# Holding SyncE's queue until a slot's diagonal blocks have landed, in a DeltaNet and attention layer

## The reference

```python
def _layer(x, w_in, conv_w, a_log, dt_bias, norm_w, sinks, w_out, ln_g, ln_b):
    h = jnp.einsum('btd,dc->btc', x, w_in)
    qa, ka, va, za, ba, aa, qb, kb, vb, zb = jnp.split(h, offsets, axis=-1)
    ya = _deltanet_group(qa, ka, va, za, ba, aa, conv_w, a_log, dt_bias, norm_w)
    yb = _swa_group(qb, kb, vb, zb, sinks)
    y = jnp.einsum('btc,cd->btd', jnp.concatenate([ya, yb], axis=-1), w_out)
    return _layernorm(DEEPNORM_ALPHA * x + y, ln_g, ln_b)

# in the DeltaNet, for each head and chunk of tokens
    a_mat = jnp.where(strict, jnp.einsum('bhncd,bhnsd->bhncs', k_beta, k) * decay, 0.0)
    t_mat = lax.linalg.triangular_solve(eye + a_mat, jnp.broadcast_to(eye, a_mat.shape),
                                        left_side=True, lower=True)
```

## Time and profile before

| | |
|---|---|
| median of 3 runs | 1107.68 us (1106.04 to 1107.72) |
| the profiled execution | 1107.0 us |
| its span, first to last instruction | 1105.1 us |
| PE busy | 1068.7 us, 97% |
| DVE, ACT, POOL busy | 690.8, 533.5, 124.4 us |
| mean granted clock | 0.997 |
| DMA moved | 183.54 MB, mean 166 GB/s |

### The profile page before, as it was taken

How to read it: one execution, slowest core, us unless ns; L and a number is a source line. 1 busy time by engine, 2 the same in 40 slices (tenths; PEclk the granted TensorE clock), 3 DMA queues, 4 the chain that set the end, 5 groups by cost and what they waited for, 6 DMA issues and landing times. The chain is left out here.

```text
span 1105.1 us, 19521 instructions
## 1 busy us (share of the span) xinstructions
PE 1068.7 (97%) x7212; PEld 851.5 (77%) x7212; DVE 690.8 (63%) x2077; ACT 533.5 (48%) x1557; POOL 124.4 (11%) x164
## 2 busy tenths in 40 slices
PE   7999999999999999999999999999999999999997
PEld 5877777867878787877877878787786868787885
DVE  5285959585565848576365765848447474758564
ACT  4466565654735444463354536444454545463310
POOL 3413222133200000020000000002000000002330
PEclk9999999999999999999999999999999999999999
DMA  8766575655652726253453461724444343612331
GB/s 274 275 245 231 205 252 201 230 182 182 224 197 85 247 81 222 95 183 101 168 190 126 155 219 53 254 78 153 147 160 153 126 153 126 228 58 60 133 113 77
DMA packets 58285, 183.54 MB, mean 166 GB/s; under 512 B 8464, under 2 KB 21200, under 8 KB 44880
## 3 DMA queue, kind: packets, MB, share of 16 engines
q1 hardware_dynamic: 51392, 173.13, 45.0%
q10 hardware_dynamic: 6800, 9.18, 2.8%
HBM read 138.22 MB, written 44.07 MB: 165 GB/s over the span
## 5 line engine op out<-in xcount | busy, mean ns | idle before, releaser
L821 PE MATMUL bank<-xr,w 128*128 128x512 f32 x2496 | 653.7, 405 | 8.7 <-DVE xr L1507 7.6
L821 PEld LDWEIGHTS bank<-xr,w 128*128 128x128 f32 x2496 | 451.7, 189 | 106.9 <-issue 13.0
L872 PE MATMUL bank<-wo,y_split 128*128 128x512 f32 x432 | 114.3, 404 | 0.0
L872 PEld LDWEIGHTS bank<-wo,y_split 128*128 128x128 f32 x432 | 77.1, 188 | 15.6 <-issue 1.7
L1555 DVE SCALAR_TENSOR_TENSOR kq<-conv_in,convw_all,kq 128x512 f32<-128x512 f32 x96 | 75.6, 787 | 9.1 <-ACT conv_in L1160 7.1
L1320 ACT ACTIVATE score<-score,neg_max 128x256 f32<-128x256 f32 (+1 forms) x128 | 62.6, 491 | 20.7 <-DVE neg_max L1725 20.7
L1879 DVE TENSOR_SCALAR steps<-bank,nb_rk 128x128 f32<-128x128 f32 x64 | 22.4, 351 | 78.0 <-PE bank L1084 78.0
L1458 ACT ACTIVATE o_scaled<-bank 128x128 f32<-128x128 f32 x64 | 17.6, 275 | 98.6 <-PE bank L1088 98.2
L1759 DVE TENSOR_TENSOR y_step<-blocks,y_cols 128x60 f32<-128x60 f32 (+14 forms) x240 | 50.5, 210 | 20.4 <-DMA blocks<-n_spill 12.0
L1882 DVE SCALAR_TENSOR_TENSOR state<-state,cols_all,bank 128x128 f32<-128x128 f32 x64 | 22.1, 345 | 60.4 <-PE bank L1087 60.3
L754 POOL TENSOR_TENSOR xr<-y_tile,xr 128x256 fp32r<-128x256 f32 x8 | 6.0, 775 | 456.7 <-ACT xr L1141 456.7
(11 more groups left out here) (218 smaller groups left out, 1642.7 us busy)
## 6 DMA issues: line engine op xcount, KB each, us to landing
w<-w_split SPq DMA_DIRECT2D x78, 1024.0 KB, 5.6
w_split<-w SPq DMA_DIRECT2D x26, 1024.0 KB, 5.3
blocks<-n_spill ACTq DMA_DIRECT2D x32, 256.0 KB
y_spill<-y_out SPq DMA_DIRECT2D x30, 256.0 KB, 4.2
x_tile<-w_in SPq DMA_DIRECT2D x13, 512.0 KB, 6.1
y_tile<-w_in SPq DMA_DIRECT2D x12, 512.0 KB, 6.5
y_tile<-y_spill SPq DMA_DIRECT2D x12, 512.0 KB, 6.7
x_tile<-x SPq DMA_DIRECT2D x12, 512.0 KB, 3.8
```

What stands on the lines that cost most here:

```text
L821: ins = nc.tensor.matmul(bank[JOBS[at].bank][:], w[:, turn % 3, wp, k, :], xr[:, xp, k], start=(step == 0), stop=(step == 3 * KT - 1))
L872: ins = nc.tensor.matmul(bank[JOBS[at].bank][:], y_place(t)[:, yp, k], wo[:, k, wp, half * UNIT:(half + 1) * UNIT], start=(step == 0), sto ...
```

## The change

In slots 5, 6, 8, 9, 10, 12, 13 and 14 (n above 4, heads 0 to 2) SP waits for one more thing before the decay rows: that the second half of this slot's blocks has landed. `blocks_in[1]` counts 16 for each slot, so the wait is for 16 (n + 1).

```diff
                 if i < AH - 1:
+                    if n > AH:
+                        after(sp, blocks_in[1], n, 16)
                     after(sp, pt_ready, n, 2)
                     load_decay(n + 1)
```

## The result

The changed kernel took **1117.27 us**, the median of 4 runs (1115.39 to 1126.46), against 1106.86 for the kernel before in 4 runs (1103.42 to 1107.72). The ratio is 1.012, with a 95% interval of 1.0087 to 1.0153: slower. The forecast was 1101.9; the rival "the tile becomes the bound" had been priced at 1116.5. The profiled execution took 1115.39 us with a span of 1113.6, 8.5 over the span before.

The account below looks back on a forecast made before the run. PE was taken as the bound, busy 97% of the span, so only its waits or clock could move the time. 5.40 for the inverse plus 0.4 for tiles gave 1107.68 - 5.8 = 1101.9 us, range 1100.3 to 1106.3.

Parts of the forecast that it names:

- the tile becomes the bound: Rival, chance 0.12: in the eight slots tiles still take 8.2 us, waits sum to about 15, less 6.2; 1116.5 us.
- What bounds the kernel, the blocks in by 4.5 us after their load: PE busy 97%, waiting for the inverse in slots 12 and 13; with SP held, blocks land 4.5 us after issue.
- The gain of 5.40 + 0.4: Inverse waits go: 1.74 us in slot 12, 3.66 in slot 13 with 1.4 for the clock; tile waits give 0.4.
- When the tile is wanted: When PE needs the weight tile: 368.5 in slot 5, 636.8 in slot 9, 842.7 in slot 12, 896.7 in slot 13.
- When the tile lands, blocks + 5.4 and blocks + 6.0: Weight tile lands 5.4 us after the blocks in slot 5 and its like, 6.0 in slots 12 and 13.
- The margins: Tile landing ahead of PE's need by 1.5, 0.9, 0.4 and 0.6 us in slots 5, 9, 12 and 13.
- it decides from about 7.1 us: Time from a tile's issue to its landing above which the slower rival, "the tile becomes the bound", decides.
- the blocks are late for another reason: Rival, chance 0.08: block loads in slots 12 and 13 are late of themselves, waits stay, no change, 1107.7 us.
- Company of the block loads: Slot 13's second block load takes 11.54 us because decay rows, tile and gated output go beside it, against 4.5 in slot 15.
- the third rival: The same as "the blocks are late for another reason"; it argued that slots 5 and 9 had the same DMAs without block waits.
- The gated output, hidden: Gated output lands around blocks + 6, near 368 in slot 5 and 895 in slot 13, before DVE's line 1748 reads it.
- The median against the profiled execution: Median of the runs taken as 0.68 us above the profiled execution, 1107.68 against 1107.0 before the change.

Follow-up runs that it names:

- number 10: Kernel before, with the tile ahead of the decay rows from slot 4 on and a hold for the blocks' first half in slots 12 to 14 alone; 1100.37 us, ratio 0.9952.
- number 7: Kernel before, with the change's hold for the second half of the blocks in slots 5, 6, 8, 9 and 10 alone; 1114.70 us, ratio 1.0081.
- number 1: The changed kernel, with the tile issued first behind the blocks in the held slots, ahead of decay rows and gated output; 1109.02 us, ratio 1.0027.
- number 8: The changed kernel, with the held slots' decay rows read from a plain 128 x 512 constant array, so those decays are zero; 1113.15 us, ratio 1.0057.
- number 9: As number 8, with the tile ahead of the gated output in slots 12 to 14; 1105.32 us, ratio 1.0002.
- number 11: Kernel before, no hold, with the decay rows issued past the middle of the slot from slot 4 on, heads 0 to 2; 1100.55 us, ratio 0.9959.
- number 2: Kernel before, with only the decay rows held for the blocks in the eight slots, tile and gated output sent ahead of that wait; 1115.18 us, ratio 1.0077.
- number 12: Number 10 and number 11 together: late decay rows, and in slots 12 to 14 the short hold with the tile first; 1100.47 us, ratio 0.9963.
- number 3: Kernel before, no hold, with the tile in the eight slots issued ahead of the pt_ready wait and the decay rows; 1110.39 us, ratio 1.0037.

## Why the prediction was wrong, step by step

- **What bounds the kernel, the blocks in by 4.5 us after their load: right but for half a us.** SP's first DMA behind the wait goes out 4.99 us after the second load in slot 5, and 4.6 to 5.3 us after it in the other seven, and line 1761 has no idle for blocks in slots 12 and 13. Both waits for the inverse are gone.
- **The gain of 5.40 + 0.4: right in cause and about in size.** The change shows it only mixed with the tile waits, but number 10 shows it alone: slots 12 and 13 last 52.05 and 51.56 us there, 2.52 and 3.67 less than before, and slot 8 0.64 less: 6.8 in the eight slots. The median fell by 4.7 only (1105.09 to 1100.37), less than in the profiled pair. Since slot 13 of number 7 was not late without any hold, the stalls of slots 12 and 13 are probably not in each run of the kernel before; the profiled run had both.
- **When the tile is wanted: right.** Slot 5's was forecast for 368.5 and PE stood ready at 369.59 - 1.59 = 368.0, in a run that is 0.7 us earlier by then.
- **When the tile lands, blocks + 5.4 and blocks + 6.0: this is the step that failed.** The term was "I take 0.6 us for each transfer of 256 KB ahead, less its head start". It came from the earlier trace rows, where the decay rows were *behind* a tile and landed 0.6 us after it. Slot 5's tile took 7.6 us, 2.6 more than the forecast 5.0. Of that, 2.1 is the decay rows ahead, for first in the same place it took 5.5 (number 1); that this is 5.5 and not 4.8 is the smaller part, 0.7. With plain rows ahead it took 5.6 (number 8), so other 256 KB ahead do cost about the 0.2 taken (0.1 to 0.4 in slots 5 to 10); it is this read that costs some ten times as much. In the last unit the gated output adds up to 2 us (numbers 8 and 9) where 0.2 was taken.
- **The margins.** They were forecast at 0.4 to 1.5 us, and each went below nothing. In slot 5 it was 1.5; less 2.6 for the tile and 0.5 for the later release that is -1.6, and PE waited 1.59. The sentence "it decides from about 7.1 us" fits in slots 5 to 10, where the tiles took 7.5 to 7.8. Slots 12 and 13 waited 1.77 and 1.98 us with only 6.7 and 7.1, since there the tile is issued some 0.6 us later after the block load than was taken, and slot 14, at 6.3, waits for 0.19 us.
- **The rival's size.** It summed to 15 us of tile waits less 6.2. That it came so near is in part luck. It took the tile's 8.2 us from a slot where blocks were beside it, and it had no term for the clock. Against number 10, slot by slot, the changed kernel is 16.1 us longer in the eight slots, of which 12.1 are tile waits. Slot 9 has 1.9 beyond its wait, where the clock fell, and each other slot 0.2 to 0.4. 16.1 less 6.8 is, but for rounding, the 9.2 of the table. Its argument against itself, "without the blocks beside it nothing explains 8 us", was the mistake: the decay rows explain it.
- **The rival "the blocks are late for another reason": wrong.** They came in time as soon as the three DMAs were held.
- **Company of the block loads.** The prediction named three DMAs as the cause of the late blocks. Holding all three did cure it, but was not needed: in number 11 output and tile beside the loads did no harm. In number 2 output and tile alone did make them late. The two differ in which side of the second load SP's first transfer was on (table under number 11). Slots 5 and 9 of the kernel before, which the third rival leaned on, had it 0.62 and 0.12 us behind.
- **The gated output, hidden: right for the change.** DVE did not wait for it in any slot. In number 1, where it stands behind tile and decay rows, it was late in slots 12 and 13, and PE waited 0.95 and 0.83 us for DVE there.
- **The median against the profiled execution.** I had them 0.7 us apart. After, the median is 1.9 above the profiled time, and the four runs reach to 1126.46 at a mean granted clock of 0.990, against 0.996 in the profiled one. Eight stalls of up to 2.0 us may give the clock more places to fall; the other three runs have no trace. The Trainium skill, "TensorE: Matmul & The Clock Gate", Part 1, says that when it changes differs from run to run. The four mean clocks, 0.996, 0.995, 0.995 and 0.990, differ too; they don't tell when it changed.

That the rows, once moved, cause no new wait was tried in two ways (numbers 10 and 11). Not tried was to move the gated output out of the crowd as well, nor to hold SP only until the second block load has been issued.

## What to carry to other kernels

A hold moves everything behind it in its queue by its own length, so ask first which single transfer of the crowd is slow, and move that one behind what is urgent: here this gave 0.9952 to 0.9963 (numbers 10 to 12; only 11 has no hold left), where holding all three gave 1.012. The price of a transfer *ahead* of another can't be read from a place where it is *behind*: look for the same pair in the same order, and if there is none, take the spread of that tile's times in the trace as the range. Hold only where the trace has a stall to remove; in the five slots where PE waited for no block, the hold cost 8.3 us of waits and won nothing.

## What the runs showed of the hardware

- A DMA that reads one DRAM row of 2 KB for all 128 partitions took 5.6 us to land in slot 5, and 2.7 for the same 256 KB from 128 different rows of another array (number 8). A 1024 KB tile right behind it took 7.6 us against 5.6. So its cost goes on to the transfer behind it; what holds it up, no run tells.
- The length of a stall of about 2 us does not tell whether the clock falls. It fell after 2.00 us in slot 9 and after 2.18 before, and PE then ran at 0.50 for the 3.3 us of each window. It did not fall after 1.99 us in slot 6, nor after 1.98 in slot 13 of the same execution. The window behind the latter:

```profile
912.20:915.50 3.30, 3.30 (x32) 2.29 (x33) 2.95 (x15) 1.05 (x5) 0.00 (x0) 1.00 0.01 5
```

- It also fell after a wait of only 1.78 us, in slot 12 of number 7, and kept its full rate after one of 2.44 us, in slot 12 of number 3. The windows behind the two, in that order:

```profile
858.60:862.00 3.40, 3.40 (x43) 2.10 (x42) 1.26 (x5) 0.28 (x1) 0.00 (x0) 0.50 0.02 5
...
846.51:849.90 3.39, 3.39 (x78) 2.44 (x79) 2.27 (x7) 0.28 (x1) 0.00 (x0) 1.00 0.05 17
```

- The fall in slot 9 cost 3.90 - 2.00 = 1.9 us beyond the wait, that in slot 13 before 3.66 - 2.18 = 1.5 (the prediction wrote 1.4).
